# Two more places and 4 MB transfers for the experts' weights in a two-block transformer kernel

## The chip, the core and the metric

The kernel runs on one core of a Trainium2 chip. The metric is the device time of one execution in microseconds (us), lower is better.

## What is computed

Two transformer blocks, 256 tokens of width 1024, in float32. Shortened from the reference:

```python
# block 1
x = x + (sigmoid(gate_a) * (moba @ w_branch_a) + sigmoid(gate_b) * (mla @ w_branch_b)) @ w_out
h = rmsnorm(x, g_ffn)                       # 256 tokens
logits = h @ w_router + b_router            # 32 experts, top 4 of them per token, softmax weights
for e in range(32):                         # rows = the tokens that chose expert e
    gu = h[rows] @ w_gate_up[e] + b_gate_up[e]          # w_gate_up[e]: 1024 x 2048
    g, u = minimum(gu[:, :1024], 7), clip(gu[:, 1024:], -7, 7)
    y = ((u + 1) * g * sigmoid(1.702 * g)) @ w_down[e] + b_down[e]     # w_down[e]: 1024 x 1024
    x[rows] += weight * y
x = x + sigmoid(rmsnorm(x, g_ple) @ w_ple_gate) * (p @ w_ple_proj)
# block 2
x = x + 0.5 * swiglu(norm(x)); x = x + mixer(norm(x)) @ w_out_2
x = x + cross_attention(norm(x), norm(mem)) ; x = x + 0.5 * swiglu(norm(x)); return norm(x) * g
```

The experts' weights are 32 x 12 MB: 8 MB for gate and up, 4 MB for down.

## The kernel before

**Parts and places.** All large weights come from memory in parts, in one fixed order that `Plan.__init__` lists. An expert has six parts of 2 MB (128 partitions x 16 KB): four of `w_gate_up` (two rows of 8 KB to a partition) and two of `w_down` (four rows of 4 KB to a partition). The order is: gate and up of expert e, sometimes a part for work that is done beside the experts, then down of expert e-1. In this text G0 to G3 of e are its four gate-and-up parts, D0 and D1 of e its two down parts, and M of e is the 1 MB part of the memory's weights (`mem_w_kv_2`, of whose 2048 columns 256 go beside each of the experts 11 to 18, the list `MEM_KV`). `Plan.place` gives each part a place in SBUF. There is a ring of `NS` = 5 places of 16 KB per partition. Part j of the ring goes to place j % 5, and its transfer is issued when the part five before it has been used. Two parts stand outside: G3 of expert 0 (`apart`) goes to the work area, and G2 of expert 1 (`spare`) goes once to `xr`, the 16 KB that held the attention's turned activations.

**Who issues.** The SP queue issues every one of these transfers (`sync`, `load_to`), in the order of the parts. Before each it waits until TensorE has done the last matmul that reads the place's former part (`e.wait_ge(*pe["w", plan.after[j]])`, line L2788 is the issue, L2782 that of `apart`). A wait holds up all later transfers. Before expert `CHECK` = 5 both TensorE and SP look at the number of tokens per expert and branch over code that is run only if an expert has more than 64 tokens (`crowded`, `spilled`); here none has.

**TensorE's order per expert n** (`tensor`, the loop over `NE`): biases (L821), gate and up of n (`gate_up`, L908, 64 matmuls), first down part of n-1, the beside work (`feat` L563 to L565, `tok_both` L592 to L594), second down part (L949), gathering of the tokens for the next group of experts (L850), a turning (L870), spreading (L859, L862) and combining (L960). Each matmul of gate and up works on 64 rows of tokens, with two running side by side on the two halves of the columns. The parts are used as they are loaded, without the high and low copies that the other weights get.

**Rows to partitions.** Partition p of a part of `w_gate_up` holds rows 2p and 2p+1 of 256 rows. The gather (`gather`, L850) takes the tokens' columns with the same step of 2.

**Other transfers.** GpSimd's queue (`gpsimd`) brings constants (L2727, L2728), biases, the router, `mem` in two halves, and `p` (L2751).

**Before the experts.** The hidden activations for the spill path (`hT32`) are multiplied by each token's norm factor: TensorE turns the factor (L839), VectorE multiplies (L2317). TensorE waits for that (`hT_n`) in expert 1.

Of the kernel before, what the change touches and what calls it, by code (L numbers as in the profile page):

```python
# [7 lines left out]
F32 = mybir.dt.float32  # L8
# [77 lines left out]
NS = 5  # L86
SLOT = 4096
PACKED = ("mem_w_kv_2", "w_ple_proj")
CHECK = 5
# [5 lines left out]
class Plan:  # L95
# [59 lines left out]

    def place(self):

        self.apart = self.of["gate_up", 0][3]
        self.spare = self.of["gate_up", 0][0] + NS + 1
        ring = [i for i in range(len(self.parts)) if i not in (self.apart, self.spare)]
        self.slot, self.after, self.load_n = ({} for _ in range(3))
        for j, i in enumerate(ring):
            self.slot[i], self.load_n[i] = j % NS, 16 * (j // NS + 1)
            self.after[i] = ring[j - NS] if j >= NS else None
        self.slot[self.spare], self.load_n[self.spare], self.after[self.spare] = NS, 16, self.of["out", 1][1]
        self.slot[self.apart], self.load_n[self.apart], self.after[self.apart] = NS + 1, 32, None

    def on_vector(self, i):

        return i != self.of["ple_gate", 0][0]

# [34 lines left out]
def build(nc, d, out, known):  # L209
# [3 lines left out]
    with ExitStack() as ctx:  # L213
# [16 lines left out]
        ring_t, ring_r = place("ring", NS * SLOT, F32, F32R)  # L230
        Wt, Wr, Wb = place("work", WN, F32, F32R, BF16)
        (x_t,) = place("xres", 2 * D, F32)
        xr_t, xr32 = place("xr", 4 * D, F32R, F32)
        (cst,) = place("cst", C_N, F32)
        (colv,) = place("colv", COL_N, F32)
        (rowv,) = place("rowv", ROW_N, F32)
# [55 lines left out]
        loaded = [sem(f"ring{i}_loaded") for i in range(NS)] + [sem("spare_loaded"), sem("apart_loaded")]  # L292
# [5 lines left out]
        def raw(i):  # L298
            return xr32[:, :] if i == plan.spare else held(ring_t, i, 0)

        def raw_chunk(i, kk):

            if i == plan.apart:
                return (W(6144, 2048), W(20288, 2048))[kk]
# [14 lines left out]
        def ready(i):  # L319

            if not parts[i].split:
                return loaded[plan.slot[i]], plan.load_n[i]
# [7 lines left out]
        o_bias = sem("o_bias")  # L330
# [5 lines left out]
        xr = xr_t[:, :].rearrange("p (s c t) -> p s c t", s=2, c=8)  # L336
# [66 lines left out]
        RSB = PS[:, LGT, 256:512]  # L403
# [21 lines left out]
        mem, mem_sq, mT = W(14336, D), W(KT, D), xT  # L425
# [85 lines left out]
        def tensor(e):  # L511
# [2353 lines left out]
```

## Time and profile before

| | |
|---|---|
| median of 3 runs | 1765.52 us (1762.68 to 1767.84) |
| profiled execution, its own time and its span | 1762.68 us, span 1762.7 us |
| TensorE matmul busy | 1643.2 us, 93% of the span |
| TensorE weight load busy | 1036.4 us, 59% |
| VectorE busy | 707.4 us, 40% |
| ScalarE busy | 571.9 us, 32% |
| GpSimd busy | 22.5 us, 1% |
| moved by DMA | 546.39 MB, 310 GB/s over the span |
| DMA issued by SP (q1) | 117344 packets, 77.4% of the 16 engines' time |
| chain that ended last | TensorE 70%, DMA 25%, VectorE 3% |

Busy time of TensorE is the union of overlapping matmuls, and not a measure of how well the array is filled. The share of busy time is an average over stages: the attention until about 190 us, the experts until about 1150 us, and the rest of both blocks after that. What bounds a stage is read from that stage alone. "DMA share" is the mean busy share of the core's 16 DMA engines; the records of packets in flight overlap a little, so that it can read 1.01.

### The profile page before, as it was taken

What the parts mean: (1) busy time and instruction counts of PE and PEld (TensorE: products, weight loads), DVE (VectorE), ACT (ScalarE), POOL (GpSimd) and SP (SyncE); (2) the same over time, 40 slices, a digit from 0 to 9 for tenths busy, and PEclk for the clock granted to TensorE, in tenths of its full rate; (3) what the DMA queues carried; (4) which work ended last, traced back from release to release, by engine and by line L of the source; (5) the groups of instructions that cost most, each with busy time, mean ns of one, the idle gap of its engine ahead of it and who ended that gap; (6) DMA issues with size and microseconds to landing.
All of it is one profiled execution on the core that took longest, in us unless ns stands there. A gap on an engine that the chain in (4) does not pass through costs nothing.

```text
span 1762.7 us, 20269 instructions
## 1 busy us (share of the span) xinstructions
PE 1643.2 (93%) x8853; PEld 1036.4 (59%) x8854; DVE 707.4 (40%) x876; ACT 571.9 (32%) x787; POOL 22.5 (1%) x37
## 2 busy tenths in 40 slices
PE   8999999898889999998888888999999999999998
PEld 7788533333235454442323232378888998988886
DVE  5897411111121211211111111167664965567663
ACT  6576200011111111100000011175563765456552
POOL 0000000000000000000000000010000000000000
PEclk9999999999999999999999999999999999999999
DMA  7538999999999999999999999955555523445552
GB/s 257 174 103 289 366 392 428 427 428 427 428 427 400 428 427 425 428 427 428 428 428 428 428 427 426 420 189 193 190 192 173 184 96 120 168 132 191 191 191 96
DMA packets 118762, 546.39 MB, mean 310 GB/s; under 512 B 5696, under 2 KB 64192, under 8 KB 92976
## 3 DMA queue, kind: packets, MB, share of 16 engines
q1 hardware_dynamic: 117344, 540.96, 77.4%
q0 software_dynamic: 1040, 4.00, 0.8%
q8 instruction: 72, 1.18, 0.3%
q14 instruction: 18, 0.15, 0.0%
q10 hardware_dynamic: 288, 0.11, 0.0%
HBM read 544.00 MB, written 1.05 MB: 309 GB/s over the span
## 4 chain that ended last, share of the span: by engine, by line
PE 70%; DMA 25%; DVE 3%; ACT 1%; issue 1%; SPq 0%; ACTq 0%
DMA ring<-in_w_down 25%; PE PS L949 10%; PE PS L908 9%; PE PS L578 8%; PE PS L1099 6%; PE PS L580 4%; PE PS L530 2%; PE PS L531 2%; PE PS L532 2%; PE PS L850 2%; PE PS L960 2%; PE PS L563 1%; PE PS L564 1%; PE PS L565 1%; PE PS L1114 1%; PE PS L549 1%
## 5 line engine op out<-in xcount | busy, mean ns | idle before, releaser
L908 PE MATMUL PS<-ring,work 128*64 128x512 f32 x2016 | 448.2, 596 | 36.5 <-DMA ring<-in_w_gate_up 36.4
L1920 DVE TENSOR_TENSOR ring<-ring,ring 128x2048 fp32r<-128x2048 f32 (+2 forms) x130 | 289.3, 2234 | 258.5 <-ACT ring L1341 258.4
L908 PEld LDWEIGHTS PS<-ring,work 128*64 128x64 f32 x2016 | 139.7, 137 | 325.4 <-issue 246.6
L1341 ACT CAST ring<-ring 128x2048 fp32r<-128x2048 f32 (+2 forms) x131 | 242.9, 1866 | 208.8 <-DMA ring<-in_mem_w_kv 86.6
L949 PE MATMUL PS<-ring,work 128*64 128x512 f32 x1024 | 239.1, 611 | 53.8 <-DMA ring<-in_w_down 37.8
L949 PEld LDWEIGHTS PS<-ring,work 128*64 128x64 f32 x1024 | 75.4, 139 | 203.5 <-issue 164.6
L2349 DVE TENSOR_SCALAR work<-PS 128x512 f32<-128x512 f32 x32 | 22.1, 690 | 325.9 <-PE PS L908 325.9
L1596 ACT ACTIVATE work<-work 128x512 f32<-128x512 f32 x32 | 20.2, 630 | 366.2 <-DVE work L2349 366.2
L2248 DVE TENSOR_TENSOR work<-PS,work 128x512 fp32r<-128x512 f32 x32 | 22.1, 692 | 252.2 <-ACT work L1540 252.2
L578 PE MATMUL PS<-xr,ring 128*128 128x512 f32 x320 | 111.2, 392 | 0.0
L578 PE MATMUL PS<-work,ring 128*128 128x512 f32 x320 | 111.2, 392 | 0.0
L1099 PE MATMUL PS<-ring,work 128*128 128x512 f32 x432 | 98.3, 390 | 0.0
L1099 PEld LDWEIGHTS PS<-ring,work 128*128 128x128 f32 x432 | 81.0, 188 | 16.8
L580 PE MATMUL PS<-work,ring 128*128 128x256 f32 x320 | 89.8, 281 | 0.0
L580 PE MATMUL PS<-xr,ring 128*128 128x256 f32 x320 | 89.8, 280 | 0.0
L1540 ACT CAST work<-PS 128x512 fp32r<-128x512 f32 x32 | 18.8, 587 | 159.5 <-PE PS L949 159.5
L578 PEld LDWEIGHTS PS<-xr,ring 128*128 128x128 f32 x320 | 59.9, 187 | 13.4 <-DVE xr L2403 0.3
L578 PEld LDWEIGHTS PS<-work,ring 128*128 128x128 f32 x320 | 59.9, 187 | 13.3 <-DVE work L2403 0.3
L530 PE MATMUL PS<-ring,xr 128*128 128x512 f32 (+1 forms) x160 | 62.7, 392 | 0.1
L531 PE MATMUL PS<-ring,xr 128*128 128x512 f32 (+1 forms) x160 | 61.7, 386 | 0.0
L532 PE MATMUL PS<-ring,xr 128*128 128x512 f32 (+1 forms) x160 | 61.7, 386 | 0.0
L580 PEld LDWEIGHTS PS<-xr,ring 128*128 128x128 f32 x320 | 60.6, 189 | 0.0
(418 smaller groups left out, 2325.1 us busy)
## 6 DMA issues: line engine op xcount, KB each, us to landing
ring<-in_w_gate_up SPq DMA_DIRECT2D x126, 2048.0 KB, 17.4
ring<-in_w_down SPq DMA_DIRECT2D x63, 2048.0 KB, 16.2
ring<-in_ffn_w_gu SPq DMA_DIRECT2D x44, 1024.0 KB, 5.1
ring<-in_w_in SPq DMA_DIRECT2D x28, 1024.0 KB, 5.4
ring<-in_ffn_w_down SPq DMA_DIRECT2D x22, 1024.0 KB, 4.9
ring<-in_w_out SPq DMA_DIRECT2D x8, 1024.0 KB, 5.6
ring<-in_mem_w_kv SPq DMA_DIRECT2D x8, 1024.0 KB, 13.8
ring<-in_w_ple_gate SPq DMA_DIRECT2D x4, 1024.0 KB, 11.6
```

The source lines that it names most:

```text
L530: e.matmul(o, lT[0][:, k, hs], whi[:, kk, :], start=k == 0, stop=False, skip_group_check=True)
L531: e.matmul(o, lT[0][:, k, hs], wlo[:, kk, :], start=False, stop=False, skip_group_check=True)
L532: t = e.matmul(o, lT[1][:, k, hs], whi[:, kk, :], start=False, stop=k == nk - 1, skip_group_check=True)
L578: e.matmul(PS[:, bank + j, :], whi[:, k, js], rT[2][:, :, k, :], start=k == 0, stop=False, skip_group_check=True)
L580: t = e.matmul(PS[:, bank + j, 0:256], wlo[:, k, js], rT[0][:, k, :], start=False, stop=k == 7, skip_group_check=True)
L850: t = e.matmul(PS[:, bank, c * 256:(c + 1) * 256], half[:, h, 256 * i + c:256 * i + 256:2], PGr[:, h, :], start=h == 0 and z == 0, stop=h ...
L908: t = e.matmul(PS[hf * 64:hf * 64 + 64, bank, :], XG[g % 2][:, 2 * kp + kk, i * 64:(i + 1) * 64], raw_chunk(w, kk)[:, c0 + hf * 512:c0 + h ...
L949: t = e.matmul(PS[dh * 64:dh * 64 + 64, BDN, :], HT[:, kk, kp * 64:kp * 64 + 64], chunks(raw(w), w)[:, kk, dh * 512:(dh + 1) * 512], start ...
L960: t = e.matmul(PS[:, BY + 2 * h + dh, :], PW[n % 2][p0:p0 + 64, h * 128:(h + 1) * 128], half[p0:p0 + 64, :], start=False, stop=False, skip ...
L1099: t = e.matmul(PS[:, 4 + 2 * h + nb, :], hT[z][:, c, hs], chunks(half, w)[:, kk, nb * 512:(nb + 1) * 512], start=c == 0 and q == 0, stop=F ...
L1341: e.copy(hi(j), raw(j)).then_inc(*act.now(("hi", j)))
L1920: e.tensor_tensor(lo(j), raw(j), hi(j).bitcast(F32), ALU.subtract).then_inc(*dve.now(("lo", j)))
```

## The change

1. `xr` becomes part of the ring's tensor, right behind place 4, and is place X: it serves every expert part from the first one that finds it free (after the last of `w_out`) up to the first part of `w_ple_gate`. A second place Y, 16 KB of the work area at 17920, serves from expert 1 until the gate and up of expert `CHECK`. `CHECK` moves from 5 to 6.
2. A part no longer goes to place j % 5 but to the place whose former part is the oldest. From expert 4 to expert 29 two gate-and-up parts (G0 with G1, G2 with G3) are loaded in one transfer of 4 MB where the two oldest places lie side by side: 48 transfers of 4 MB, the remaining 8 parts as before. Such a transfer waits for both places, and both parts share one semaphore.
3. For all experts, partition p of gate and up now holds rows 4p to 4p+3 of 512 rows. The joined transfer reads 32 KB in one piece per partition; a single one reads 16 KB out of each 32 KB. `gather`, the gain `g_ffn_pairs` and the split of `normed_rest` follow.
4. `apart` is issued right after the first part of expert 0 and no longer waits for `bias_2`.
5. The multiplication of `hT32` and the turning of the factor are gone from the usual path; the spill path makes its activations itself.
6. The memory's turned activations `mT` leave `xr` and lie in pieces in free corners (`more`, `cst`, `rowv`, the work area). So the second half of the constants (512 KB) and `p` (256 KB) are loaded after the last memory part of expert 18.

```diff
-CHECK = 5
+X, Y, APART = NS, NS + 1, NS + 2
+CHECK = 6
+JOINED, FIRST_JOINED = ('w_gate_up',), 4
...
+        held = {s: s - NS for s in range(NS)}
+        i = 0
+        while i < len(self.parts):
+            if i == first:
+                held[X], held[Y] = self.of["out", 1][1] - 0.5, self.of["out", 1][1] + 0.5
+            if i == crowded:
+                del held[Y]
+            if i == behind:
+                del held[X]
+            oldest = sorted(held, key=held.get)
+            slots = oldest[:1]
+            if i == self.apart:
+                slots = [APART]
+            elif self.joined(i) and max(oldest[:2]) <= X and abs(oldest[0] - oldest[1]) == 1:
+                slots = sorted(oldest[:2])
+            after = [held[s] for s in slots if held.get(s, -1) >= 0]
...
-            e.wait_ge(*dve["factor_out"])
-            for h in range(2):
-                t = e.matmul(RSB[:, h * 128:(h + 1) * 128], rn[:, h:h + 1].to_broadcast([128, 128]), ident, start=True,
-                             stop=True, skip_group_check=True)
-            t.then_inc(*pe.now("rsb"))
...
-            e.wait_ge(*pe["rsb"])
-            e.tensor_tensor(hT32, hT32, bc(RSB, [128, 8, 256], 1), ALU.mult).then_inc(*dve.now("hT_n"))
...
-            e.dma_start(cst[:, C_HM:C_N], d["cst"][:, C_HM:C_N]).then_inc(hm_in, 16)
...
-                if g == 1:
-                    e.wait_ge(*pe["comb", 0])
+                if g == 5:
+                    e.wait_ge(*pe["beside", MEM_KV[-1]])
                     e.dma_start(p_raw, d["p"].rearrange("(h p) n -> p h n", p=128)).then_inc(p_in, 16)
+                    e.dma_start(cst[:, C_HM:C_N], d["cst"][:, C_HM:C_N]).then_inc(hm_in, 16)
...
-                    if plan.after[j] is not None:
-                        e.wait_ge(*pe["w", plan.after[j]])
+                    for k in after:
+                        e.wait_ge(*pe["w", k if k in plan.slot else of["out", 1][1]])
...
+                    elif p.name == "w_gate_up":
+                        r0, k0 = p.k0 // 4 * 512, p.k0 % 4
+                        src = w[p.expert][r0:r0 + 512, :].rearrange("(p k) n -> p k n", p=128)[:, k0:k0 + n * p.k, :]
...
-                        e.wait_ge(*act["bias_2", 64])
...
+                    elif n == 2:
+                        s = plan.slot[j]
+                        e.dma_start(ring_t[:, s * SLOT:(s + 2) * SLOT].rearrange("p (k n) -> p k n", n=p.n),
+                                    src).then_inc(in_memory(j)[0], 16)
                     else:
+                        if plan.slot[j] == Y:
+                            e.wait_ge(*pe["logits"])
+                            e.wait_ge(*act["bias_2", 64])
```

On the SP queue, from the second part of expert 0 to the down parts of expert 1, the order was (`ring_49` is the ring, `xr_56` the spare, `work_51` the work area):

```order
L2782 DMA work_51<-in_w_gate_up 128x2048 x2
L2788 DMA ring_49<-in_w_gate_up 128x4096 x2
L2788 DMA xr_56<-in_w_gate_up 128x4096
L2788 DMA ring_49<-in_w_gate_up 128x4096
L2788 DMA ring_49<-in_w_down 128x4096 x2
L2788 DMA ring_49<-in_w_gate_up 128x4096 x4
L2788 DMA ring_49<-in_w_down 128x4096 x2
```

and is now, up to the first joined transfers of experts 4 and 5:

```order
L2834 DMA work_51<-in_w_gate_up 128x2048 x2
L2847 DMA ring_49<-in_w_gate_up 128x4096 x5
L2847 DMA work_51<-in_w_gate_up 128x4096
L2847 DMA ring_49<-in_w_down 128x4096 x2
L2847 DMA ring_49<-in_w_gate_up 128x4096 x4
L2847 DMA work_51<-in_w_down 128x4096
L2847 DMA ring_49<-in_w_down 128x4096
L2847 DMA ring_49<-in_w_gate_up 128x4096 x4
L2847 DMA ring_49<-in_w_down 128x4096
L2847 DMA work_51<-in_w_down 128x4096
L2841 DMA ring_49<-in_w_gate_up 128x8192 x2
L2847 DMA ring_49<-in_w_down 128x4096 x2
```

The `apart` pair stood behind three ring parts and stands behind one; the last of expert 1's gate-and-up parts goes to Y in the work area instead of the ring, and then every part finds a place that is seven parts old instead of five. Two 128x4096 parts became one 128x8192 transfer from expert 4 on.

## Rows read from the trace of the kernel before

**Rows 1.** Busy in stretches: PE, PEld, DVE, ACT, POOL, PEclk, DMA share, GB/s.

```profile
160.00:255.00 95.00, 94.22 (x479) 51.18 (x480) 38.64 (x74) 23.69 (x35) 3.44 (x5) 0.96 0.94 373
255.00:520.00 265.00, 227.94 (x1137) 86.33 (x1135) 49.23 (x94) 34.29 (x64) 2.90 (x5) 0.98 1.01 427
520.00:525.00 5.00, 5.00 (x15) 1.49 (x12) 0.23 (x1) 0.00 (x0) 0.00 (x0) 0.57 1.04 436
525.00:535.00 10.00, 10.00 (x69) 7.34 (x69) 0.00 (x0) 1.14 (x2) 0.00 (x0) 1.00 0.81 310
535.00:1120.00 585.00, 524.12 (x2759) 224.10 (x2760) 98.46 (x152) 63.89 (x100) 4.68 (x8) 1.00 1.01 427
```

**Rows 2.** TensorE's waits from 290 to 1120 us: total us, times, longest.

```profile
PE PS L908 <- DMA ring<-in_w_gate_up: 36.4, 36, 1.3
PE PS L949 <- DMA ring<-in_w_down: 35.1, 27, 3.8
```

**Rows 3.** The chain that ended last, at the last experts: start, us, what.

```profile
1118.49 12.49 DMA ring<-in_w_down
1131.11 5.35 PE PS L949 x16
```

**Rows 4.** DMA issues of the whole execution: KB each, median us to landing.

```profile
ring<-in_ffn_w_gu SPq DMA_DIRECT2D x44, 1024.0 KB, 5.1
cst<-in_cst POOLq DMA_DIRECT2D x1, 512.0 KB, 9.3
work<-in_p POOLq DMA_DIRECT2D x1, 256.0 KB, 5.2
```

**Rows 5.** SP's queue, experts 0 and 1: start, us, issue.

```profile
158.21 12.13 SPq L2788 DMA_DIRECT2D ring<-in_w_gate_up  x3
...
182.18 0.43 SPq L2788 DMA_DIRECT2D xr<-in_w_gate_up  x1
196.72 0.33 SPq L2788 DMA_DIRECT2D ring<-in_w_gate_up  x1
201.46 5.07 SPq L2788 DMA_DIRECT2D ring<-in_w_down  x2
215.42 17.09 SPq L2788 DMA_DIRECT2D ring<-in_w_gate_up  x4
235.62 9.15 SPq L2788 DMA_DIRECT2D ring<-in_w_down  x2
```

**Rows 6.** TensorE in the same stretch: start, us, matmuls.

```profile
188.29 1.22 PE L839 MATMUL PS<-cst,stat 128*128 128x128 f32 x4
...
211.78 7.03 PE L908 MATMUL PS<-ring,work 128*64 128x512 f32 x32
...
223.05 3.60 PE L908 MATMUL PS<-ring,work 128*64 128x512 f32 x16
...
228.49 7.09 PE L949 MATMUL PS<-ring,work 128*64 128x512 f32 x32
...
240.79 13.90 PE L908 MATMUL PS<-ring,work 128*64 128x512 f32 x64
```

**Rows 7.** VectorE's multiplication that goes: start, us, operation.

```profile
194.28 2.28 DVE L2317 TENSOR_TENSOR work<-work,PS 128x2048 f32<-128x2048 f32 x1
```

**Rows 8.** TensorE at expert 11's memory part: start, us, matmuls, idle before.

```profile
518.24 6.63 PE L949 MATMUL PS<-ring,work 128*64 128x512 f32 x16 [3.79 <-DMA ring<-in_w_down]
524.80 0.39 PE L563 MATMUL PS<-xr,ring 128*128 128x256 f32 x1
...
530.75 3.65 PE L949 MATMUL PS<-ring,work 128*64 128x512 f32 x16
```

**Rows 9.** DMA queue from 780 to 1000 us: packets, MB, share of 16 engines.

```profile
q1 hardware_dynamic: 6450, 93.90, 100.4%
```

**Rows 10.** The same, 560 to 740 us.

```profile
q1 hardware_dynamic: 5686, 76.60, 100.3%
```

**Rows 11.** TensorE at the check before expert 5.

```profile
326.40 1.06 PE L821 MATMUL PS<-work,selb 96*64 96x512 bf16 x4 [7.60 <-issue]
```

More of the change, by code:

```diff
@@ L154, in ffn, with joined @@
             self.add((f, "down", k), [(f + "_w_down_2", 2 * k, 2, 0, 1024)])
+    def joined(self, i):
+        p = self.parts[i]
+        if p.name not in JOINED or not FIRST_JOINED <= p.expert < NE - 2:
+            return False
+        return (p.k0 // p.k) % 2 == 0
     def place(self):
+        first, crowded, behind = (self.of[k][0] for k in (("gate_up", 0), ("gate_up", CHECK), ("ple_gate", 0)))
         self.apart = self.of["gate_up", 0][3]
-        self.spare = self.of["gate_up", 0][0] + NS + 1
@@ L163, in place @@
[L163 to L169, printed above, removed]
+        self.slot, self.at, self.loads = {}, {}, []
@@ new lines, in place @@
+        count = dict.fromkeys(range(APART + 1), 0)
+        held = {s: s - NS for s in range(NS)}
[14 more added lines that the diff above has]
+            after = [held[s] for s in slots if held.get(s, -1) >= 0]
+            count[slots[0]] += 32 if i == self.apart else 16
+            for k, s in enumerate(slots):
+                self.slot[i + k], self.at[i + k] = s, (slots[0], count[slots[0]])
+                if s != APART:
+                    held[s] = i + k
+            self.loads.append((i, len(slots), after))
+            i += len(slots)
@@ L171, in on_vector, with __init__, __getitem__ @@
+        early = next(n for n in self.loads if n[0] == self.apart)
+        self.loads.remove(early)
+        self.loads.insert(1 + [n[0] for n in self.loads].index(first), early)
     def on_vector(self, i):
         return i != self.of["ple_gate", 0][0]
+class Chunks:
+    def __init__(self, chunks):
+        self.chunks = chunks
+    def __getitem__(self, at):
+        p, k, cols = at
+        return self.chunks[k][p, cols]
 class Count:
@@ L289, in stats, with in_memory @@
             return stat[:, o:o + n]
[L292 removed]
+        loaded = [sem(f"ring{i}_loaded") for i in range(NS)] + [sem(f"{n}_loaded") for n in ("place_x", "place_y", "apart")]
+        def in_memory(i):
+            return loaded[plan.at[i][0]], plan.at[i][1]
         def held(t, i, o):
@@ L1007, in crowded @@
                 with e.If(most > CAP):
+                    for c in range(8):
+                        for h in range(2):
+                            o = PS[:, 4 + c // 2, (c % 2) * 256 + h * 128:(c % 2) * 256 + h * 128 + 128]
+                            for half in (hnh, hnl):
+                                m = e.matmul(o, half[:, h, c * 128:(c + 1) * 128].bitcast(F32), ident, start=half is hnh,
+                                             stop=half is hnl, skip_group_check=True)
+                    m.then_inc(o_turned, 1)
+                    e.wait_ge(o_normed, 1)
                     with e.Fori(0, NE) as n:
@@ L2279, in crowded @@
                 with e.If(most > CAP):
+                    e.wait_ge(o_turned, 1)
+                    for c in range(8):
+                        t = e.tensor_scalar(hT32[:, c, :], PS[:, 4 + c // 2, (c % 2) * 256:(c % 2) * 256 + 256],
+                                            gain("g_ffn", c), None, ALU.mult)
+                    t.then_inc(o_normed, 1)
                     with e.Fori(0, NE) as n:
```

62 lines of the change are left out of this document (32 added, 30 removed).

## The prediction

> **What bounds the kernel now.** I read four views in order. The table of stretches comes first [rows 1]: from 255 to 1120 us, over the experts, the 16 DMA engines are full (share 1.01, 427 GB/s), while TensorE is busy 228 of 265 us and 524 of 585 us. TensorE's waits agree [rows 2]: they end on weights that land, seldom over 1.3 us. The chain of waits hangs on the last down weights, and then on TensorE [rows 3]; no wait of that size on a transfer follows. So the experts cost the bytes over the rate, and a change counts for as much as it brings forward the landing of expert 31's weights. Two stretches of the stream are not full: 160 to 255 us (373 GB/s) and 525 to 535 us (310 GB/s) [rows 1]. At 427 GB/s the first lacks (1 - 373/427) x 95 = 12.0 us of transfer, the second (1 - 310/427) x 10 = 2.7 us.
>
> **Two more places at the head.** A 2 MB part (2.097 MB) takes 4.91 us at 427 GB/s. A lone 1 MB transfer lands 5.1 us after its issue [rows 4], 2.5 us of them for its bytes, so I give an issue about 2.4 us before its bytes move. Before the change the queue stands because each part needs the place of the part five before: G3 of expert 1 is issued at 196.7, G0 of expert 2 at 215.4, and D1 of expert 1, the last of 235.62 + 9.15, at 244.4 [rows 5]. That last one moves from 246.8 to 251.7; afterwards the queue is always ahead of the engines.
>
> After the change I take TensorE's times as they stand, since it has no gap there (94.2 of 95 us busy [rows 1]). Transfers start at 160.6 us (issue at 158.2 [rows 5]) and chain: G0 and the early G3 of expert 0, G1, G2, then G0, G1, G2 and G3 of expert 1. G3 no longer waits for 196.7; its place Y asks for the router's logits, which are done by 188.3, when L839 runs [rows 6]. Eight parts end at 199.9. D0 and D1 of expert 0 need what was given back at 196.7 and 201.5 [rows 5], and end at 209.7. G0 of expert 2 needs the place that D1 of expert 0 took before, given back at 206.2 (201.46 + 5.07 less the issue), and ends at 214.6. G1 of expert 2 needs G0 of expert 1, done halfway in the 7.03 us from 211.78 [rows 6], at 215.3: its bytes begin at 217.7, 3.1 us of standing. The next four follow without a gap, since they need what is done at 218.8, 223, 226.7 and 232 [rows 6]: D1 of expert 1 ends at 217.7 + 5 x 4.91 = 242.3. That is 9.4 us earlier than 251.7. The other parts then need places seven parts old. Bounds: 12.0 us (no gap left) and 6 us (a first 4 MB transfer that stands up to 3.1 us for its second place, like the gap just found). I take **9.0 us**, near the schedule, because TensorE (228 of 265 us busy from 255 us on) has slack to give places back.
>
> L839 (1.22 us, 4 matmuls) and the multiplication on VectorE (2.28 us) leave the head [rows 6, 7]. They stand ahead of the first gate-and-up matmuls, so places are given back at most 1.2 us earlier; nothing downstream of a full stream gains. I count it at 0, the bound is +1.2.
>
> **The hole at 525 us.** D0 of expert 10 waits 3.79 us and then runs mostly at the lower clock of 1.2 GHz (granted 0.57 of full from 520 to 525 us [rows 1]; 6.63 us for 16 matmuls that take 3.65 us), the memory part M runs from 524.80 to 530.75, and only then is its place free [rows 8]. Four transfers (19.6 us) separate M from the part that takes its place, before and after the change alike. The 3.79 us come because G3 is done just when the 1 MB of M and the 2 MB of D0 (7.4 us) have still to land. With G2 and G3 in one transfer TensorE has 7.1 us of work at that landing (7.09 us for two down parts, 7.03 for two gate-and-up parts [rows 6]), so the idle time before D0 shrinks to 0.3 us, and I expect D0 to run at 2.4 GHz. M still waits for D0, but it is done 6.63 - 3.65 = 3.0 us sooner after its landing, more than the hole is long. The hole goes: **2.7 us**, bounds 0 and 2.7.
>
> **The 4 MB transfers.** 48 transfers of 4 MB replace 96 of 2 MB. From 780 to 1000 us, 93.90 MB in 6450 packets fill 100.4% of 16 x 220 us, 37.64 us of engine per MB [rows 9]; from 560 to 740 us, where each expert has 1 MB in rows of 8 KB, it is 100.3% of 16 x 180 for 76.60 MB, 37.71 us [rows 10]. The packets per MB are 68.7 and 74.2, so a packet costs (37.71 - 37.64) / 5.5 = 13 ns, an estimate at the edge of what the shares resolve. If 32 KB go as one packet, a joined transfer saves 128 packets and 16 semaphore packets: 144 x 13 ns / 16 = 0.12 us, times 48 is 5.6 us. I take **5.0 us**, bounds 0 (the row is cut at 16 KB) and 8 (20 ns a packet).
>
> A first rule to weigh: the rate shows that chained transfers pay no fixed cost between them, since 2.097 MB / 427 GB/s is all that one takes [rows 1]. The Trainium skill, page "SBUF — State Buffer", section "The DMA setup-cost knee", gives 2 us plus bytes / 436 GB/s per transfer and advises the largest single transfer; by that 48 fewer would save 96 us. The trace's 427 GB/s at 2 MB speaks against it for a queue that is always ahead.
>
> What the 4 MB transfers cost: TensorE gets G0 only with G1, 4.9 us later. In a plain expert it is idle (1 - 228/265) of 29.5 us, 4.1 us, which now falls into two waits instead of five. Its work per expert does not grow, and the stream stays the bound. Both places of a joined part have been read long before: six places hold 29.5 us of transfer, and 7.1 us of matmuls after a landing leave over 9 us of margin. In the rounds with M the margin is 0 to 2.5 us, the same as before, as M's place is again four transfers away.
>
> **The rest.** 0.52 MB of constants and 0.26 MB of `p` [rows 4] move into the full stream: 0.79 MB / 427 GB/s = 1.8 us lost. The check before expert 6 makes TensorE idle 7.60 us as the one before expert 5 did [rows 11]; there the DMA stayed at 427 GB/s [rows 1], and the queue has one place more now. Price 0, at most 3 us if G1 of expert 6 is given back late. The gather, the biases and the end are the same work.
>
> **Sum.** -9.0 - 2.7 - 5.0 + 1.8 = -14.9 us. The profiled execution (span 1762.7, time 1762.68) becomes 1747.8; the median of the runs is 2.8 us above it, so 1765.5 - 14.9 = **1750.6 us**.
>
> **Rivals.**
> A. Rows of 32 KB bring nothing, since the rate is a ceiling of the engines and not a matter of packets. For it: the rate is 427 GB/s with and without the 8 KB rows [rows 1, 9, 10], and my 13 ns is small. Time: 1765.5 - 9.9 = 1755.6. The Trainium skill, page "DMA: Bandwidth & Descriptors", section "Measured (HBM→SBUF, 128 partitions, SWDGE, issued from GpSimd)", has 425 GB/s at 16 MB, the rate of this trace at 2 MB, which would put it on this side.
> B. The lead is lost: the first 4 MB transfer and the check take 3 us each, and the hole stays. Against it: the margins above. Time: 1765.5 - 9 - 5 + 1.8 + 6 = 1759.3, and with A too 1764.3, the same as before.
> C. Slower: the second place comes late in the eight memory rounds. There a run of D0 at 1.2 GHz costs 3.0 us (6.63 against 3.65 [rows 8]), SP stands for it with every later transfer behind it, and margins are near 0. If TensorE's waits, now fewer and longer (2 to 2.7 us), bring the lower clock in each round, 8 x 3.0 = 24 us are lost: 1765.5 - 14.9 + 24 = 1774.6. It decides against the change from 2.6 us a round. Against it: one of eight rounds showed it, after the longest wait of all, 3.79 us [rows 2, 8].
> D. The change does not do what it says: rows of 32 KB slow the engines. From 427 to 405 GB/s on the 201 MB of joined parts is +25 us, 1775. No row speaks for it.
>
> **Chances and numbers.** A measurement of this kernel tells 0.3% (5.3 us) from no change. My forecast 0.55, A 0.25, B 0.10 (half of it within 5.3 us), C 0.05, D 0.05. Faster 0.83, same 0.08, slower 0.09. The range runs from 1743 (12.0 at the head, 8 for packets, 2.7, less 1.8, and 1.2 for L839, with some of it missed) to 1760 (B).
>
> **What would show it.** D1 of expert 1 issued by about 232 instead of 244 us; DMA at 427 or more from 218 us; no dip near 515 us; packets from 780 to 970 us fewer per MB and the rate at 430 to 431 GB/s (A: 427). The last down weights land some 15 us earlier, and everything from there has its old length. I am wrong if the stream shows new holes at joined issues, if PEclk falls in many rounds, or if the time after the last landing changes.

## The result and the profile after

| | before | after |
|---|---|---|
| median | 1766.68 us (1762.68 to 1768.15, 4 runs) | 1757.71 us (1756.04 to 1759.17, 4 runs) |
| span of the profiled execution | 1762.7 us | 1757.2 us |
| packets | 118762 | 111850 |

The ratio is 0.9955, 95% interval 0.994 to 0.997: faster by some 8 us (5 to 11 us by the interval), where 14.9 were forecast. The time lies inside the range, 7 us above the forecast.

The stretches of the changed kernel, columns as in [rows 1]:

```profile
160.00:255.00 95.00, 93.30 (x449) 52.77 (x449) 35.06 (x70) 23.72 (x35) 2.35 (x4) 0.95 0.95 390
255.00:520.00 265.00, 247.53 (x1190) 100.59 (x1187) 51.01 (x94) 34.45 (x64) 2.88 (x5) 0.96 1.00 427
520.00:525.00 5.00, 5.00 (x39) 4.00 (x39) 0.00 (x0) 0.59 (x1) 0.00 (x0) 1.00 1.02 426
525.00:535.00 10.00, 10.00 (x58) 5.32 (x54) 2.17 (x5) 1.55 (x3) 1.18 (x2) 1.00 0.97 409
535.00:1120.00 585.00, 540.92 (x2746) 238.00 (x2744) 99.05 (x147) 63.60 (x98) 4.79 (x8) 0.99 1.00 428
```

The hole at 525 us is nearly gone (409 against 310 GB/s), and the stream afterwards is a shade faster (428). But the head reached only 390 GB/s, 17 more than [rows 1], which is 17/427 x 95 = 3.8 us of the 9.0 forecast. The SP queue shows where it stands (start, us, issue):

```profile
198.00 5.98 SPq L2847 DMA_DIRECT2D ring<-in_w_down  x2
209.33 18.29 SPq L2847 DMA_DIRECT2D ring<-in_w_gate_up  x4
230.73 0.33 SPq L2847 DMA_DIRECT2D work<-in_w_down  x1
236.22 0.33 SPq L2847 DMA_DIRECT2D ring<-in_w_down  x1
```

D1 of expert 1 is issued at 236.2, not at the forecast 232 (before at 244.4 [rows 5]). Nothing of the queue is slow. It waits for TensorE, and TensorE is later than in [rows 6] (start, us, matmuls):

```profile
189.06 4.15 PE L890 MATMUL PS<-work 128*128 128x256 f32 x16 [1.01 <-DVE work L2281]
193.14 4.82 PE L948 MATMUL PS<-ring,work 128*64 128x512 f32 x16
197.89 2.14 PE L890 MATMUL PS<-work 128*128 128x256 f32 x8
199.96 3.65 PE L948 MATMUL PS<-ring,work 128*64 128x512 f32 x16
...
215.82 7.03 PE L948 MATMUL PS<-ring,work 128*64 128x512 f32 x32
...
245.77 4.46 PE L948 MATMUL PS<-ring,work 128*64 128x512 f32 x20
```

Gate and up of expert 1 starts at 215.82 instead of 211.78, of expert 2 at 245.77 instead of 240.79. Eight matmuls of a gather (L890) take 2.14 us. Before they took 1.23:

```profile
196.60 1.23 PE L850 MATMUL PS<-work 128*128 128x256 f32 x8
```

The cause is the load of the stationary operand. One line's view shows the ns as min/median/max, first of the kernel before, then of the changed one:

```profile
L850 PEld LDWEIGHTS PS<-work x256: 192/196/331, 189.2 to 1019.6; 128*128 128x128 f32 x128
L850 PE MATMUL PS<-work x256: 278/283/552, 189.2 to 1019.7; 128*128 128x256 f32 x128
```

```profile
L890 PEld LDWEIGHTS PS<-work x256: 307/330/338, 189.0 to 1015.0; 128*128 128x128 f32 x128
L890 PE MATMUL PS<-work x256: 390/396/570, 189.1 to 1015.1; 128*128 128x256 f32 x128
```

With a step of 4 floats between columns the load takes 330 ns instead of 196, and the matmul behind it 396 instead of 283. The Trainium skill, page "Advanced Engine Details and Errata", section "SBUF Cachelines", says that SBUF has lines of 16 bytes and that a reader needs at least two hits on one to hide the access time. The trace agrees: a step of 2 floats hits each line twice, a step of 4 once.

D0 of expert 10, which waited 3.79 us and ran for 6.63 us in [rows 8], now runs without a wait at full clock, as forecast:

```profile
514.04 3.60 PE L989 MATMUL PS<-ring,work 128*64 128x512 f32 x16
```

The DMA queue from 780 to 1000 us, against [rows 9]: two thirds of the packets, and 0.6% more bytes, 94.44/220 = 429 GB/s (the forecast had 430 to 431).

```profile
q1 hardware_dynamic: 4320, 94.44, 100.2%
ring<-in_w_gate_up SPq DMA_DIRECT2D x15, 4096.0 KB, 22.0
```

The check, now before expert 6, is as in [rows 11]. But this time the stream has a dip around it (columns as above):

```profile
353.23 1.06 PE L867 MATMUL PS<-work,selb 96*64 96x512 bf16 x4 [7.84 <-issue]
```

```profile
350.00:360.00 10.00, 6.77 (x20) 2.43 (x22) 0.04 (x1) 0.35 (x1) 0.00 (x0) 0.53 0.97 410
360.00:365.00 5.00, 5.00 (x26) 1.82 (x24) 0.00 (x0) 0.00 (x0) 0.00 (x0) 1.00 1.07 423
365.00:375.00 10.00, 10.00 (x50) 3.53 (x47) 2.73 (x4) 0.96 (x3) 0.00 (x0) 1.00 0.93 393
```

That is (17 + 34)/427 x 10 = 1.2 us, plus less than 0.1. Of TensorE's waits the view reads, against [rows 2]:

```profile
PE PS L948 <- DMA ring<-in_w_gate_up: 43.6, 25, 2.7
PE PS L989 <- DMA ring<-in_w_down: 7.8, 8, 2.0
```

Fewer waits, each up to 2.7 us, as forecast. The granted clock falls a little: 0.96 from 255 to 520 us and 0.99 later, against 0.98 and 1.00. The landing of the last down weights, against [rows 3], and the end of the chain:

```profile
1124.41 3.65 PE L989 MATMUL PS<-ring,work 128*64 128x512 f32 x16 [1.99 <-DMA ring<-in_w_down]
```

```profile
L624 PE MATMUL PS<-work,ring 128*128 128x512 f32 x320 | 113.3, 399 | 0.0
L624 PE MATMUL PS<-ring 128*128 128x512 f32 x320 | 111.2, 392 | 0.0
```

The last down matmuls start 6.7 us sooner (1124.41 against 1131.11), and run at full clock. Behind them one of the two feed-forwards took 2.1 us longer: its 320 matmuls of 512 columns averaged 399 ns, where both had 392 before.

### The profile page after: what moved, and what is told of

It is laid out like the page before. It is cut to its first block, busy times and chain, and to the rows that moved or that the text cites. A ratio compares the mean times of both kernels' runs of the same rounds, so it can differ in the third digit from the quotient of the medians.

```text
span 1757.2 us, 20261 instructions
## 1 busy us (share of the span) xinstructions
PE 1672.6 (95%) x8849; PEld 1064.1 (61%) x8850; DVE 708.7 (40%) x873; ACT 572.9 (33%) x787; POOL 22.1 (1%) x37
## 2 busy tenths in 40 slices
DMA packets 111850, 546.39 MB, mean 311 GB/s; under 512 B 4928, under 2 KB 63424, under 8 KB 92208
## 4 chain that ended last, share of the span: by engine, by line
PE 68%; DMA 28%; DVE 3%; ACT 1%; issue 1%; DVEq 0%; SPq 0%; ACTq 0%
DMA ring<-in_w_gate_up 18%; PE PS L948 14%; DMA ring<-in_w_down 9%; PE PS L624 8%; PE PS L989 6%; PE PS L1146 6%; PE PS L626 4%; PE PS L576 2%; PE PS L578 2%; PE PS L577 2%; PE PS L890 1%; PE PS L609 1%; PE PS L610 1%; PE PS L611 1%; PE PS L1161 1%; DMA ring<-in_w_ple_gate 1%
## 5 line engine op out<-in xcount | busy, mean ns | idle before, releaser
L948 PE MATMUL PS<-ring,work 128*64 128x512 f32 x2000 | 456.7, 612 | 43.6 <-DMA ring<-in_w_gate_up 43.6
L989 PE MATMUL PS<-ring,work 128*64 128x512 f32 x992 | 222.8, 595 | 9.9 <-DMA ring<-in_w_down 9.8
L624 PE MATMUL PS<-ring 128*128 128x512 f32 x320 | 111.2, 392 | 0.0
L626 PE MATMUL PS<-ring 128*128 128x256 f32 x320 | 89.6, 280 | 0.0
L890 PEld LDWEIGHTS PS<-work 128*128 128x128 f32 x256 | 62.3, 328 | 24.6 <-issue 23.5
L890 PE MATMUL PS<-work 128*128 128x256 f32 x256 | 68.7, 413 | 1.0 <-DVE work L2281 1.0
L624 PEld LDWEIGHTS PS<-ring 128*128 128x128 f32 x320 | 59.9, 187 | 13.5 <-DVE ring L2452 0.3
L576 PE MATMUL PS<-ring 128*128 128x512 f32 (+1 forms) x160 | 62.7, 392 | 0.2 <-DVE ring L1967 0.2
L577 PE MATMUL PS<-ring 128*128 128x512 f32 (+1 forms) x160 | 61.7, 386 | 0.0
L578 PE MATMUL PS<-ring 128*128 128x512 f32 (+1 forms) x160 | 61.6, 385 | 0.0
```

Of the source, the lines that this page charges most:

```text
L576: e.matmul(o, lT[0][:, k, hs], whi[:, kk, :], start=k == 0, stop=False, skip_group_check=True)
L577: e.matmul(o, lT[0][:, k, hs], wlo[:, kk, :], start=False, stop=False, skip_group_check=True)
L578: t = e.matmul(o, lT[1][:, k, hs], whi[:, kk, :], start=False, stop=k == nk - 1, skip_group_check=True)
L624: e.matmul(PS[:, bank + j, :], whi[:, k, js], rT[2][:, :, k, :], start=k == 0, stop=False, skip_group_check=True)
L626: t = e.matmul(PS[:, bank + j, 0:256], wlo[:, k, js], rT[0][:, k, :], start=False, stop=k == 7, skip_group_check=True)
L890: t = e.matmul(PS[:, bank, c * 256:(c + 1) * 256], half[:, h, 512 * (i // 2) + 2 * (i % 2) + c:512 * (i // 2) + 512:4], PGr[:, h, :], star ...
```

## How the runs are read

Two measures stand beside each other. The median of the runs against before's tells what a kernel is worth; its interval is about 0.13% (2.3 us) to each side, so single differences of 2 us need support. The trace of one execution tells where. Three marks of it serve below: the start of gate and up of expert 2 (the head), the MB that the SP queue had moved by 1100 us (before: 421.26), and the start of the last down matmuls (before: 1131.11).

| kernel | ratio to before, 95% interval | median us | gather's load ns | expert 2 at | MB by 1100 us | last down at |
|---|---|---|---|---|---|---|
| before | 1 | 1764.6 to 1766.7 | 196 | 240.79 | 421.26 | 1131.11 |
| changed | 0.9955 [0.994, 0.997] | 1757.71 | 330 | 245.77 | 423.67 | 1124.41 |
| changed, again | 0.9959 [0.9944, 0.9973] | 1758.03 | 330 | 243.84 | 424.67 | 1122.46 |
| new rows alone | 1.0036 [1.0022, 1.0049] | 1770.99 | 330 | 244.73 | 418.96 | 1136.33 |
| places alone | 0.9963 [0.995, 0.9975] | 1758.32 | 195 | 240.82 | 425.34 | 1123.08 |
| places, five after the check | 0.9949 [0.9935, 0.9962] | 1757.07 | 195 | 242.49 | 424.16 | 1124.52 |
| joined, two rows | 0.9953 [0.9938, 0.9968] | 1757.86 | 195 | 240.49 | 423.46 | 1125.37 |
| changed, not joined | 0.9975 [0.9966, 0.9984] | 1760.51 | 329 | 243.27 | 424.64 | 1124.64 |
| turned store | 0.9937 [0.9921, 0.9952] | 1753.86 | 189 | 243.46 | 424.26 | 1124.09 |
| turned store, again | 0.9938 [0.9924, 0.9951] | 1755.28 | 188 | 241.28 | 424.78 | 1123.01 |
| turned, joined late | 0.995 [0.9936, 0.9963] | 1755.91 | 189 | 243.28 | 424.59 | 1123.24 |
| turned, not joined | 0.9965 [0.9952, 0.9978] | 1758.77 | 189 | 242.32 | 424.85 | 1124.44 |
| two rows, then four | 0.9951 [0.9938, 0.9965] | 1756.68 | 193, then 329 | 242.52 | 425.09 | 1121.61 |

Two cautions on "expert 2 at". The attention ahead ends up to 3 us earlier or later in one profile than in another (the first gather starts between 187.5 and 191.3 us). And the turned kernels add some 1.5 us of their own: from the matmuls of L852, which turn `x`, to the first gather they take 9.5 us, the change 8.0 and 7.8. Counted from the first gather, expert 2 starts after 51.6 us before, after 51.1 to 52.6 in all kernels with a load under 200 ns, and after 55.4 to 56.7 in all with 330 ns.

The medians carry noise too. By the intervals of the ratios, a difference of two kernels in the table can be off by 2.4 to 3.4 us either way.

## The experiments

**The turned store.** What the changed kernel would be if its gather read neighbouring floats. `hnh` and `hnl` are written so that the four classes of columns lie apart:

```diff
-half[:, h, 512 * (i // 2) + 2 * (i % 2) + c:512 * (i // 2) + 512:4]
+half[:, h, (2 * i + c) * 128:(2 * i + c + 1) * 128]
...
-e.activation(hnh[:, h, :], x[:, h, :], ACT.Identity, scale=rn[:, h:h + 1])
+e.activation(hnh[:, h, :].rearrange("q (b k p) -> q b k p", b=2, k=4), x[:, h, :].rearrange("q (b p k) -> q b k p", b=2, k=4),
+             ACT.Identity, scale=rn[:, h:h + 1])
```

> Theory G (the gather's weights, now read with a step of 4 floats, made TensorE later at the head, and with it the places that are given back): with the same values stored so that the gather reads neighbouring floats, the weight load falls from 330 ns to 196 ns or less, expert 2 starts 3 to 4 us earlier than in the changed kernel, and the time is 3 to 4 us below it, ratio to the kernel before 0.993. Rival H (the longer spell at 1.2 GHz at the head did it): the load falls, but expert 2 starts within 1.5 us of the changed kernel's and the time stays at 0.995 to 0.996. Rival K (a full stream hides the head): time unchanged though expert 2 starts earlier.

Measured: ratio 0.9937. The load is at 189 ns:

```profile
L890 PEld LDWEIGHTS PS<-work x256: 186/189/333, 191.3 to 1014.0; 128*128 128x128 f32 x128
```

The gather's load is dear only by its step. The two medians of this kernel (here, and again below) are the lowest of the table, 3.4 us ahead of the change's two, give or take 2.6 us. Expert 2 starts 2.3 us earlier than in the change, not 3 to 4, because the turned store has a price of its own: ScalarE, which now reads `x` with a step of 4 floats, takes 4.12 us for the two writes of `hnh` and not 2.18, and the first gather waits for what follows. First the change, then this kernel:

```profile
183.94 2.18 ACT L1574 ACTIVATE work<-xres,stat 128x1024 fp32r<-128x1024 f32 x2
```

```profile
184.72 4.12 ACT L1574 ACTIVATE work<-xres,stat 128x1024 fp32r<-128x1024 f32 x2
```

The last down matmuls do not show the lead: they start at 1124.09 and 1123.01 us in the two profiles of this kernel, at 1124.41 and 1122.46 in the change's.

**The change without joined transfers.** `JOINED` is empty; rows of four, places and all else stay.

```diff
-JOINED, FIRST_JOINED = ('w_gate_up',), 4
+JOINED, FIRST_JOINED = (), 4
```

> The change without the 4 MB transfers, rows still four to a partition. Theory J (a joined transfer saves 0.1 us of the engines' time): 48 x 0.1 = 5 us slower than the changed kernel, ratio to before 0.998. Rival L (what the packets save is lost again, because TensorE gets its weights later and gives them back in pairs): within 1.5 us of the changed kernel, 0.995 to 0.996. Rival M: faster than the changed kernel, if the pairs cost more than they save.

Measured: ratio 0.9975, 3.2 us slower than the change's two medians, give or take 2.4 us, between what J and L give. The spell at the lower clock at the head is shorter here: the stretch from 180 to 205 us, first of the change, then of this kernel (PEclk is the third number from the end).

```profile
180.00:205.00 25.00, 23.30 (x117) 15.57 (x116) 11.28 (x39) 6.83 (x11) 1.18 (x2) 0.80 1.01 407
```

```profile
180.00:205.00 25.00, 23.30 (x124) 15.54 (x124) 11.97 (x40) 6.83 (x11) 1.17 (x2) 0.86 1.00 414
```

Yet the second profile of the change (below) has 0.86 as well, as the kernel before has: the spell differs between executions of one kernel.

**The places alone.** Two rows to a partition, step 2, no joined transfer: only the places and what moved with them.

```diff
-half[:, h, 512 * (i // 2) + 2 * (i % 2) + c:512 * (i // 2) + 512:4]
+half[:, h, 256 * i + c:256 * i + 256:2]
...
-JOINED, FIRST_JOINED = ('w_gate_up',), 4
+JOINED, FIRST_JOINED = (), 4
```

> The places, the moved loads and the dropped multiplication alone: two rows to a partition, gather with a step of 2, no 4 MB transfers. Theory G: the head is as early as forecast, expert 2 starts within 1 us of the kernel before, and it is 3 to 4 us faster than the run with four rows and no joined transfers. With J this gives a ratio to before of 0.995 to 0.996, about the same as the changed kernel: the two halves of the change would cancel. Rival K: equal to the run with four rows and no joined transfers.

Measured: ratio 0.9963. Its SP queue in the head:

```profile
226.72 0.33 SPq L2848 DMA_DIRECT2D work<-in_w_down  x1
232.21 0.33 SPq L2848 DMA_DIRECT2D ring<-in_w_down  x1
```

D1 of expert 1 is issued at 232.2, as the forecast's schedule had it. The stretches confirm the rest:

```profile
160.00:255.00 95.00, 93.30 (x465) 49.60 (x465) 34.12 (x71) 23.48 (x35) 2.35 (x4) 0.95 0.98 406
520.00:525.00 5.00, 5.00 (x30) 2.48 (x28) 0.00 (x0) 0.59 (x1) 0.00 (x0) 1.00 1.01 429
525.00:535.00 10.00, 10.00 (x62) 4.86 (x62) 2.02 (x5) 1.55 (x3) 1.18 (x2) 1.00 1.01 425
```

The hole is gone, with no joined transfer in the kernel. And TensorE waits before D0 of expert 10 as in [rows 8]:

```profile
509.12 6.56 PE L989 MATMUL PS<-ring,work 128*64 128x512 f32 x16 [3.81 <-DMA ring<-in_w_down]
...
521.55 3.65 PE L989 MATMUL PS<-ring,work 128*64 128x512 f32 x16
```

So the hole closes without the forecast's reason: here the late D0 stays, and the sixth place covers it. By 1100 us the queue had moved

```profile
q1 hardware_dynamic: 41806, 425.34, 92.6%
```

and before

```profile
q1 hardware_dynamic: 41525, 421.26, 92.1%
```

4.08 MB more, 9.6 us at 427 GB/s; the forecast for head, hole and moved loads is 9.0 + 2.7 - 1.8 = 9.9. But the last down matmuls start 8.0 us sooner, not 9.6, and the median gains 6.5.

**Joined transfers with two rows.** Both parts in one transfer of 4 MB, but in pieces of 16 KB, and step 2.

```diff
-e.dma_start(ring_t[:, s * SLOT:(s + 2) * SLOT].rearrange("p (k n) -> p k n", n=p.n),
+e.dma_start(ring_t[:, s * SLOT:(s + 2) * SLOT].rearrange("p (j n) -> p j n", j=2),
```

> 4 MB transfers with the old rows, two pieces of 16 KB per partition and a gather with a step of 2. If the gain of a joined transfer is that of fewer packets, it has none here: equal to the run with the places alone, within 1 us, packets of 16 KB. If it is that of fewer transfers (48 fewer semaphores, one queue entry less): 1 us or more faster than the places alone. By rival L it is slower than the places alone.

Measured: ratio 0.9953, 1.8 us ahead of the places alone, give or take 3.4 us, so not to be told from them; its last down matmuls start 2.3 us later. From 780 to 1000 us its queue reads

```profile
q1 hardware_dynamic: 6217, 94.01, 100.4%
```

A larger transfer with as long pieces moves as much as 2 MB transfers do (93.97 MB in the places alone). The gain in rate belongs to the pieces of 32 KB. The dip at the check is largest here, 249 GB/s from 360 to 365 us.

**The new rows alone.** The kernel before with rows of four and the gather's step of 4, five places, no joined transfer.

```diff
-half[:, h, 256 * i + c:256 * i + 256:2]
+half[:, h, 512 * (i // 2) + 2 * (i % 2) + c:512 * (i // 2) + 512:4]
...
-c0, c1 = ((0, 256), (256, 512), (512, D))[part]
+c0, c1 = ((0, 512), (512, D))[part]
```

> The kernel before with only the new rows of gate and up and what follows from them (the gather's step of 4 floats, the gain, the split of normed_rest): five places, no 4 MB transfer. Theory G (the gather is dearer by itself): the gather's weight load is about 330 ns instead of 196, its matmul 396 instead of 283, a gather 0.9 us longer; the first two groups lie where places must be given back, so the parts of experts 0 to 2 land 1.8 to 2 us later than before, and the median is 1 to 2.5 us above that of before. Rival S (the step only costs in the changed kernel, since its head has no slack): before, TensorE waits for weights in the head anyway, and the median is within 0.5 us of before. Rival P (16 KB read out of each 32 KB slows the stream): the rate over the experts falls below 427 GB/s and more than 4 us are lost.

Measured: ratio 1.0036, 6 us slower than before and more than twice what theory G gave; the last down matmuls start 5.2 us later. The stretches:

```profile
160.00:255.00 95.00, 94.25 (x459) 53.82 (x459) 37.62 (x71) 23.97 (x36) 3.06 (x5) 0.96 0.90 354
255.00:520.00 265.00, 237.37 (x1150) 95.69 (x1146) 45.96 (x89) 32.41 (x63) 2.89 (x5) 0.98 1.00 425
```

The head falls from 373 to 354 GB/s, 19/427 x 95 = 4.2 us, about the 3.9 us by which expert 2 starts later. With five places the head's loss reaches the queue in full. By 380 us the queue has lost another 1.3 us (52.76 MB from 255 to 380 us, before 53.30), which the head does not account for and no run takes apart. P is out: from 780 to 1000 us this queue moves 93.90 MB in 6451 packets, as [rows 9]. S is out too.

**The changed kernel again**, with no edit.

> The changed kernel once more, unaltered. It shows how far two profiled executions of one kernel lie apart. Theory G says that its gate and up of expert 2 starts between 243 and 246 us, by the length of the low-clock spell in the head (3.3 us apart between 6.8 and 10.2), and that the median is 1756 to 1759, ratio 0.994 to 0.997. Theory H (the joined parts lengthen the spell): 10.2 us again and 245.8. The 512-column matmuls of the second feed-forward at the end take 391 or 399 ns: 399 again if it belongs to the kernel, either of them if it belongs to the execution.

Measured: ratio 0.9959. The granted clock from 180 to 205 us was 0.86, expert 2 at 243.84, and 424.67 MB were moved by 1100 us, 1.0 more than in the first profile. H falls. So one profile of this kernel lies 2 us beside another, and every figure that is read from one profile carries that. Most of it is not the clock: the first gather starts 1.5 us earlier here, and only the other 0.4 us arise between it and expert 2. The slow 512-column matmuls changed places: here it was the first feed-forward that took 399 ns. They belong to the execution and not to the kernel.

**The turned store with joined transfers from expert 7 on.**

```diff
-JOINED, FIRST_JOINED = ('w_gate_up',), 4
+JOINED, FIRST_JOINED = ('w_gate_up',), 7
```

> The turned store with joined transfers only from expert 7 on, so that none is issued around the check of the tokens per expert. Theory K (a joined transfer waits for two places behind the check, and the stream has a hole of 1.3 us or more at 360 us): the hole goes, 1.0 to 1.5 us sooner from there on, less 6 joined transfers at 0.08 (0.5 us): 0.5 to 1 us faster than the turned store alone, 1753.2. Rival L: another wait takes the hole's place and the time is that of the turned store, or 0.5 us above it.

Measured: ratio 0.995, against 0.9937 and 0.9938: no gain, if anything a loss. Its last down matmuls start at 1123.24, beside 1124.09 and 1123.01. It has 43 joined transfers. From 340 to 380 us the stream does not lose the 1.0 to 1.2 us that it loses in the two turned kernels with all 48 (17.22 MB, there 16.52 and 16.61; before 17.04), so theory K has the hole right. But rival L has the time right: what is saved at the check is not seen in the end.

**The turned store without joined transfers.**

```diff
-JOINED, FIRST_JOINED = ('w_gate_up',), 4
+JOINED, FIRST_JOINED = (), 4
```

> The turned store without any joined transfer. If 48 joined transfers save 0.08 us each and lose 1.3 us at the check, this is 2.5 us slower than the turned store with them (1756.4). Theory J (0.1 us each, loss at the check made good by other things): 3 to 5 us slower. Rival L (the joined ones' saving is given back): within 1 us of it.

Measured: ratio 0.9965, 4.9 us (0.28% of 1765) behind the mean of the two turned ones with joined transfers. With rows of four and the strided gather the same step was 3.2 us (0.9975 against 0.9957). The pair of pairs puts 48 joined transfers at 3 to 5 us (give or take 2.4 and 2.9), 0.07 to 0.10 us each, and the strided gather at 3.4 us with them (0.9957 against 0.9938, give or take 2.6) and 1.8 without (0.9975 against 0.9965, give or take 2.8, so by itself not clear of zero).

**Two rows first, then four.** Experts 0 to 7 as before the change, four rows and joined transfers from expert 8 on.

```diff
+half[:, h, 256 * i + c:256 * i + 256:2] if g < 2 else
 half[:, h, 512 * (i // 2) + 2 * (i % 2) + c:512 * (i // 2) + 512:4]
...
-elif p.name == "w_gate_up":
+elif p.name == "w_gate_up" and p.expert >= 8:
...
-JOINED, FIRST_JOINED = ('w_gate_up',), 4
+JOINED, FIRST_JOINED = ('w_gate_up',), 8
```

> The changed kernel with two rows to a partition (gather step 2) for experts 0 to 7 and four rows, the gather step of 4 and joined transfers from expert 8 on. Theory G (the step of 4 costs where the gather stands in the head, and nothing where the stream is full): the head is that of the kernel with the places alone (gate and up of expert 2 at 240.8), the later gathers keep their load of 330 ns without costing anything, and 44 joined transfers save 0.07 us each, 3 us: ratio 0.9935, some 1753.5 where before is 1765. Rival L (the gather costs wherever it stands, since TensorE's later landings of places hold up joined transfers): no faster than the change, 1757 to 1758.

Measured: ratio 0.9951. The kernel has 41 joined transfers, not the 44 of the expectation. By the trace G holds: 51.8 us from the first gather to expert 2, the most bytes of all joined kernels by 1100 us, the earliest last landing (1121.61). By the median L is nearer: 1756.7 against its 1757, and the interval of the ratio, 0.9938 to 0.9965, ends just short of G's 0.9935. The trace and the median do not agree, and which of the two theories holds stays open.

**Seven places in the head, five after the check.** The places alone, and both extra places go at the check.

```diff
             if i == crowded:
-                del held[Y]
+                del held[Y], held[X]
```

> The kernel with the places alone (two rows, no joined transfer), but with five places again from the check before expert 6 on; the head keeps seven. Theory X (the sixth place closed the hole at 525 us, not the joined transfer): the hole returns, 520 to 535 us is at about 350 GB/s instead of 415, and the bytes after it are 2.6 us later: 2 to 3 us slower than the places alone, ratio 0.9975 to 0.998. Theory S (a sixth place also makes each transfer of a full stream land later after its issue, 25 us instead of 20.8, and that delays the last landing by 1.6 us): that part comes back, the last down matmuls start as early as with six places, and the time is within 1 us of the places alone. Theory J (the joined G2 and G3 closed the hole and the places did not): the hole is unchanged against the places alone.

Measured: ratio 0.9949, at least as fast as with the sixth place (0.9963). The stretch and the queue from 780 to 1000 us:

```profile
520.00:525.00 5.00, 5.00 (x29) 2.36 (x27) 0.00 (x0) 0.58 (x1) 0.00 (x0) 1.00 0.88 338
525.00:535.00 10.00, 10.00 (x62) 4.96 (x62) 2.02 (x5) 1.54 (x3) 1.17 (x2) 1.00 1.00 426
```

```profile
q1 hardware_dynamic: 6457, 94.00, 100.4%
ring<-in_w_gate_up SPq DMA_DIRECT2D x30, 2048.0 KB, 20.7
```

The hole returns in part: 89/427 x 5 = 1.0 us, where before had 2.7. Here D0's run after the wait took 5.00 us, not 6.63, which may be why; X is right in kind and half in size, and the 2 to 3 us that it gave are not in the median. Of S, the shorter time to landing holds: a transfer lands 20.7 us after its issue, where the places alone have

```profile
ring<-in_w_gate_up SPq DMA_DIRECT2D x31, 2048.0 KB, 25.1
```

With five places 2.90 MB more than before (6.8 us) turn into 6.6 us at the last down matmuls. With six, 4.08 MB (9.6 us) turn into 8.0, and the two other kernels with six places and single transfers lose as much (7.9 us into 6.5, 8.4 into 6.7). With the sixth place some bytes are moved sooner without a transfer being done sooner. The kernels with joined transfers do not lose it: the change's bytes lie 5.6 and 8.0 us ahead, its last down matmuls 6.7 and 8.6. What makes a landing later than the bytes say, the view of the queue does not tell, and no run tests it. Here the last down matmuls start 1.4 us later than in the places alone; the first gather did so by 1.6.

**The turned store again**, with no edit.

> The turned store once more, unaltered, for a comparison on the same chip with the kernel of two rows first. If its lead is its own, the ratio to before is 0.9925 to 0.995 again and 2.5 to 4 us better than the change's 0.9955 and 0.9959; if the first result was a matter of the day, 0.995 to 0.996.

Measured: ratio 0.9938, median 1755.28, 1.4 us ahead of the kernel of two rows first on the same chip. The lead of the medians over the change came back. No trace shows it at the last landing.

## Why the prediction was right or wrong

The direction and the reason for it hold: the experts cost the bytes over the rate, and the bytes came sooner. The size was 7 us off. Two measures share that out. By the medians, the path places alone (0.9963), rows of four (0.9975), joined (mean of 0.9955 and 0.9959) is 6.5 - 2.1 + 3.2 = 7.6 us, where the forecast had 9.9 + 0 + 5.0. By the start of the last down matmuls the same path is 8.0 - 1.6 + 1.2 = 7.7 us. The sums agree. The shares differ by up to 2 us, within that scatter: the places fall short by 3.4 or 1.9 us, the gather costs 2.1 or 1.6, the joined transfers miss 1.8 or 3.8.

The bytes tell in which stretch. The table has what the SP queue moved more than before in each, in us at 427 GB/s (0.1 us is 0.04 MB):

| stretch, us | forecast | places alone | changed, not joined | changed | changed, again |
|---|---|---|---|---|---|
| to 160 | 0 | 1.3 | 1.3 | 0.3 | 1.7 |
| 160 to 255, the head | 9.0 | 7.9 | 6.1 | 4.5 | 5.1 |
| 255 to 500 | part of 5.0 | -0.3 | -0.2 | 0.0 | 0.5 |
| 500 to 540, the hole | 2.7 | 2.7 | 2.8 | 2.0 | 1.6 |
| 540 to 700 | part of 5.0 | 0.1 | -0.1 | -0.1 | 0.0 |
| 700 to 780, the moved loads | -1.8 | -2.0 | -1.8 | -1.5 | -1.8 |
| 780 to 1100 | part of 5.0 | -0.2 | -0.1 | 0.5 | 0.8 |
| by 1100 | 14.9 | 9.6 | 7.9 | 5.6 | 8.0 |

- **"The gather, the biases and the end are the same work."** This step failed outright: it put at nothing a cost that has a size. The change's own list names the gather, and the prediction looked at its count of matmuls and not at its operand. Its load went from 196 to 330 ns, a gather from 1.23 to 2.15 us. Six of them stand on TensorE before expert 2. The last four cost 0.9 us more each, some 3.7 us, exactly where the queue waits for places, and no cover was left there: TensorE was busy 94.2 of 95 us [rows 1]. In the head's bytes the kernels with a step of 2 gain 7.3 to 9.4 us, the turned ones 6.6 to 7.7, those with a step of 4 only 4.5 to 6.1. At the end of the kernel it is 1.6 to 3.4 us, so the gather explains between a quarter and a half of the 7 us.
- **The head, 9.0 us.** The schedule was right as a schedule: with the old gather D1 of expert 1 is issued at 232.2, the head gains 7.9 us on a queue that was already 1.3 us ahead, and 9.6 us of bytes lie ahead at 1100 us, hole and moved loads included. What failed with the places alone is the last link, from bytes to time: bounds 6 to 12 took bytes for landings. With six places and single transfers of 2 MB 1.4 to 1.7 us of the lead are not in landings. A further 1.5 us lies between the last landing (8.0) and the median (6.5), inside the interval and the difference of two profiles. (The prediction's time from an issue to the first byte is 5.1 - 2.5 = 2.6 us by its own numbers, not 2.4. It enters both schedules, so the lead hardly changes.)
- **The hole, 2.7 us.** Right in size with single transfers, and not for the reason given. It closes with no joined transfer, while D0's wait (3.81 us) and its low clock stay: with six places of which the oldest is taken, five transfers separate M from the part that takes its place, not four. In the changed kernel D0's wait does go, as forecast, and four is right, since G2 and G3 in one transfer take M's place. There SP stands 12.4 us for M's last matmul, L611 (its waits from 470 to 530 us), and 0.7 to 1.1 us of the hole are left in the two profiles:

```profile
SPq L2821 <- PE PS L611: 12.4, 1, 12.4
```

- **The 4 MB transfers, 5.0 us.** The mechanism held as to the rate: fewer packets per MB, not larger transfers. By the queue of the two profiles the change moved 0.54 and 0.39 MB more in 220 us with 15 joined transfers, 1.3 and 0.9 us, so 0.06 to 0.08 us each, not 0.12. Times 48 that is 3 to 4 us. But the stream gives nearly all of it back where a joined transfer waits for its second place, at the check and at the hole: from 255 to 1100 us the change gains 0.8 and 1.2 us over before, the same kernel without joined transfers 0.5 us. With the turned store it is 0.4 and -0.8 against 0.5. The wait for a second place was the second step that failed: the prediction gave it over 9 us of margin, and in the rounds with M no more than before, and so no price. The last landings are 1.2 and 0.9 us earlier with joined transfers, the medians 3.2 and 4.9 us, clear of zero. Where the rest of the medians' gain arises, no run shows. Rival A (nothing) falls for the rate and the medians, not for the bytes moved by 1100 us.
- **The check, at most 3 us.** 1.2 us in the first profile, and 1.0 and 1.2 with the turned store. That part of rival B came true. But joined transfers that begin behind the check did not win it back at the end.
- **Rival C**: the granted clock did fall in more places (0.95 to 0.97 from 255 to 520 us in the change and the turned store with joined transfers, 0.97 to 0.98 without them), and the last landing was not later for it. **Rival D** falls with the 428 GB/s.
- **The moved loads, 1.8 us**: right. From 700 to 780 us the SP queue of every kernel with the change's places loses 1.4 to 2.4 us against before, and that of the rows alone 0.1. The 0.79 MB stand in the other queue (690 to 790 us of the changed kernel):

```profile
q0 software_dynamic: 224, 0.79, 2.0%
```

- **"Everything from there has its old length."** Not in the profile (2.1 us longer in one feed-forward), but the same kernel shows it now in one stage and now in the other, so it is no cost of the change.

## What to carry to other kernels

A layout that is changed for the sake of DMA packets changes the step of every other reader of that index. List the readers and price each operand's load at its new step before calling the rest the same work. At a step of one float in four TensorE's stationary load took two thirds longer here (330 against 196 ns), and it cost most where a queue stood for that engine. When a stream bounds a stage, look at landings and not at bytes alone: with a sixth place and single transfers 1.4 to 1.7 us of the bytes' lead were in no landing. And when a transfer is made larger so that it needs two places, look for the rounds in which the second place comes late: here those rounds took back nearly all that the longer pieces saved in bytes.

## What the runs showed of the hardware

- The load of a 128x128 float32 stationary operand took 189 ns with neighbouring floats, 196 at a step of 2, 330 at a step of 4; the 256-column matmul behind it 283, 283 and 396 ns.
- Reading 16 KB out of each 32 KB of memory cost the stream nothing: 93.90 MB in 220 us both ways.
- Transfers of 4 MB in pieces of 32 KB moved 0.3 to 0.6% more in the same time than pieces of 16 KB did, and 4 MB in pieces of 16 KB no more than 2 MB (94.01 MB in 220 us against 93.90 to 94.00).
- ScalarE's two operations over 128x1024 float32 took 2.18 us reading neighbouring floats and 4.12 us reading with a step of 4 floats.
- A feed-forward's 320 matmuls of 512 columns average 392 to 394 ns or 399 ns, for a whole stage at a time, and the choice differs between executions of one kernel, at a granted clock of 1.00. That is 2 us per stage, a good part of the scatter of the runs. No run here tells why.
